# A two-layer decoder step on one core: sums of squared head outputs as two fp32r products, half tiles moved behind each output step, state buffers laid into dead memory, one subtraction moved ahead

## The chip, the cores and the metric

One core of a Trainium2 chip runs the whole program in one launch. The metric is device time in microseconds (us); each figure below is for that one core. The engines are named as the profile names them: PE is the matmul engine (PEld its weight loads), DVE the vector engine, ACT the scalar engine, POOL the general engine, SP the one that issues most loads.

## The reference

A decoder of two layers, each a half-step SwiGLU FFN, a mixer of three recurrent branches, and another half-step FFN. It is computed for one prompt of 512 tokens and for 8 running sequences of 4 new tokens, 544 token columns in all. The part of the mixer that the change touches:

```python
def head_rmsnorm(o, g):
    return o * lax.rsqrt(jnp.mean(o * o, axis=-1, keepdims=True) + EPS) * g

# per branch (HGRN2, GLA, mLSTM), 4 heads of 128 values each:
#   S_t = diag(exp(logf_t)) S_{t-1} + k_t v_t^T ;  o_t = S_t^T q_t
o_hg  = merge_heads(head_rmsnorm(o_hg,  g_hgrn)) * silu(hg)
o_gla = merge_heads(head_rmsnorm(o_gla, g_gla))  * silu(gg)
o_ml  = merge_heads(head_rmsnorm(h_ml,  g_ml))   * sigmoid(mo)
proj   = einsum('blcw,cwd->blcd', branches, w_branch[l])
merged = einsum('blcd,blcd->bld', sigmoid(mg), proj);  y = merged @ w_out[l]

def swiglu_half(x, g, w_up, w_down):
    gate, up = split(rmsnorm(x, g) @ w_up)
    return x + 0.5 * ((silu(gate) * up) @ w_down)
```

The running sequences bring a state (8 x 128 x 128 for each head of HGRN2 and mLSTM, two heads together for GLA), which is read, updated and written back.

## The kernel before

Activations lie transposed, 128 channels on the partitions and 544 token columns, which are treated as two halves of 272. **Dense products** (`dense`, L700) take three fp32r products for each 128x128 weight block: rounded weight by rounded activation, rounded weight by the activation's rest, the weight's rest by the rounded activation. A tile of the mixer has 8 blocks, so 48 matmuls of 272 columns; half a tile ("part") has 24. POOL splits each piece of weights into rounded part and rest (L567, L569), SP loads it. Two PSUM slots `dense` are used in turn; ACT or DVE empties a tile and gives its slot back (`slot_free`).

**The mixer's order** is one list, `ORDER`, that every engine walks. `mixer_order` makes it with `weave`: the recurrent steps of a branch, and behind each step so many half tiles of dense work as `HALVES_BEHIND` says (one row of numbers for each branch). PE starts a step only when DVE and ACT have finished the step before (`dve_step`, `act_step`); the half tiles between are the cover for their work. For each of 4 heads a branch ends with two steps:
- **o**, the output step: PE makes the head's outputs into PSUM `SA` (L972 to L976). ACT copies them to memory and squares them into `tmp[:, 2]` (L1355 to L1359). DVE makes `vblk` (L2028) and the next head's queries `qm` (L1913), and in the mLSTM branch adds a lower bound to the squares (L2037).
- **z**: PE makes the state update of the running sequences (L981, L984), then the sums of the squares over the 128 partitions by a product with `ones` in plain fp32 (L988), and, but for the last head, reads the next head's states (L817, L819). ACT takes Ln and Exp of the sums (L1382, L1385). DVE updates the state `sst` (L2042, L2044), then tells `dve_step`, then scales the outputs (L2050, L2052, L2054) with a copy by ACT between (L1394). DVE and ACT do all this in program order, and a gate's tile that ACT empties (L1260, Sigmoid) needs a table load before it, as Ln does after it.

That makes 24 o steps and 24 z steps (2 layers, 3 branches, 4 heads).

**States.** The 10 states of a layer pass through four buffers `sst0` to `sst3` (`st_buf`, `st_count`). A buffer is loaded again behind the o step once the store of its last state has landed.

**The start of an FFN** (f = 0 to 3, two for each layer). FFN 0 runs its tiles as dense products, with some replaced; FFNs 1 to 3 make nearly all tiles by seven half-size products (`fast`, L760), which need sums and differences of the activations: `combined` (L1601 to L1608), rounded by ACT (L1112, `combined_hi`) and their rest by DVE (L1612, `combined_lo`), in two groups, 0 and 1. PE's second product in `fast` waits for both rests. Between the two `combined_lo` DVE does `hidden_lo` (L1633) and `gate_scaled(2, 1)` (L1619), which empties PSUM slot 0 of the third tile. ACT's Silu (L1126) follows `gate_scaled`; then DVE `gate` (L1623) and `value` (L1628), ACT's copy to `Ah` (L1130), and ACT's copy of the first product (L1087), for which PE's fourth product waits. In FFN 0 the fifth tile of dense products uses slot 0 again.

Of the kernel before, what the change touches and what calls it, by code (L numbers as in the profile page):

```python
# [22 lines left out]
ALU = mybir.AluOpType  # L23
ACT = mybir.ActivationFunctionType

P = 128
# [76 lines left out]
def scan_steps(br):  # L103
# [135 lines left out]
def build(nc, wst, xT, par_d, lb_d, const_d, lvm_d, fg_d, st_h, st_g, st_c, st_n, st_m,  # L239
          yT, p_h, p_g, p_c, p_n, s_h, s_g, s_c, s_n, s_m, x_keep):  # L240
    ctx = ExitStack()
    with ctx:
        top = [(nc.sbuf_base + 31) // 32 * 32]

        def sb(name, shape, dt=F32, at=None):
# [3 lines left out]
            if at is None:  # L249
# [23 lines left out]
        tmp, tmp_at = sb("tmp", [P, 6, TOK])  # L273
        vblk, _ = sb("vblk", [2 * SMP, 512], at=tmp_at + 3 * TOK * 4)
# [29 lines left out]
        sst = [sb("sst0", [P, DEC_B, P])[0], sb("sst1", [P, DEC_B, P], at=tmp_at)[0],  # L304
               sb("sst2", [P, DEC_B, P], at=b_at + 4 * TOK * 4)[0], sb("sst3", [P, DEC_B, P], at=b_at + 6 * TOK * 4)[0]]
# [89 lines left out]
        den_sq, num_sq = sem("den_sq"), sem("num_sq")  # L395
        h_rs, h_of, h_hi, h_lo = sem("h_rs"), sem("h_of"), sem("h_hi"), sem("h_lo")
# [29 lines left out]
        def st_buf(n):  # L426

            return n % 2 if n < 7 else (2, 3, 1)[n - 7]

        def st_count(L, n):  # L430

            return L * (64, 64, 16, 16)[st_buf(n)] + 16 * (n // 2 + 1 if n < 7 else (1, 1, 4)[n - 7])
# [252 lines left out]
        def _(pe):  # L685
# [124 lines left out]
            def state_query(L, br, h, out):  # L810

                n = st_no(br, h)
                pe.wait_ge(st_in[st_buf(n)], st_count(L, n))
                pe.sem_inc(step_began, 1)
                for b in range(DEC_B):
                    j = b % 4
                    pe.matmul(out[j * SMP:(j + 1) * SMP, :], qm[:, b * SMP:(b + 1) * SMP], sst[st_buf(n)][:, b, :],  # L817
                              start=(b < 4), stop=(b > 4), skip_group_check=True)
# [11 lines left out]
            def step(L, s):  # L830
# [146 lines left out]
                elif kind == "z":  # L977
# [51 lines left out]
        def _(act):  # L1029
# [184 lines left out]
            def tile(L, t):  # L1214
# [42 lines left out]
                elif t in GATE_AT:  # L1257
                    m = GATE_AT[t][1]
                    tile_wait(L, t)
                    act.activation(halves(gates[:, m, :]), ps, ACT.Sigmoid).then_inc(free, 1)  # L1260

            def dma_state(L, i, store):
# [7 lines left out]
                if store:  # L1270
                    act.dma_start(v(d[0]), sst[st_buf(i)][:, :, :]).then_inc(st_out[st_buf(i)], 16)
                else:
                    act.dma_start(sst[st_buf(i)][:, :, :], v(d[1])).then_inc(st_in[st_buf(i)], 16)
# [15 lines left out]
            def step(L, s):  # L1289
# [31 lines left out]
                elif kind == "k":  # L1321
# [11 lines left out]
                    else:  # L1333
# [4 lines left out]
                        if br < 2:  # L1338
                            ch.did(act.activation(kts[:, 0:nt, :].rearrange("p a b -> p (a b)"),
                                                  SA[0:2 * SMP, 0, 0:nt * P], ACT.Copy))  # L1340
                elif kind == "ns":
# [8 lines left out]
                elif kind == "o":  # L1350
                    if br == 2:

                        act.activation(tmp[:, 2, 0:SEQ], SA[:, 0, :], ACT.Square).then_inc(num_sq, 1)
                        act.activation(tmp[:, 2, SEQ:TOK], SA[:, 1, 0:SMP], ACT.Square).then_inc(num_sq, 1)
# [7 lines left out]
                    n = st_no(br, h)  # L1362
# [4 lines left out]
                    if (br, h) == (1, 3):  # L1367
# [914 lines left out]
```

## Time and profile before

| | us |
|---|---|
| median of 3 runs | 2925.52 |
| lowest, highest | 2921.17, 2928.85 |
| the profiled execution | 2927.8 |
| its span, first to last instruction | 2926.0 |
| PE busy in the span | 2893.3 |
| DVE busy | 1634.6 |
| POOL busy | 1589.8 |
| ACT busy | 925.9 |

The span is cut into work of the engines. PE is busy nearly throughout, the others half the time or less. The mean granted clock of PE was 0.994 of full speed. The views used below are the page, the waits (who waited for whom), the timeline (instructions in order of time, alike ones merged), the list of a line's instructions, the windows (busy time of each engine in a stretch, with the granted clock) and the chain of work that ended last.

### The profile page before, as it was taken

The page shows a single profiled execution, that of the slowest core. Times are in us where ns is not written, and L with a number is a line of the kernel's source. Part 1 is how long each engine was busy: PE and PEld are TensorE (multiplying, and loading weights), DVE is VectorE, ACT ScalarE, POOL GpSimd, SP SyncE. Part 2 cuts the span into 40 slices and gives each one's busy share as a digit, 9 for nine tenths or more (in the row PEclk, how much of TensorE's full clock was granted, in tenths as well). Part 3 has the DMA queues.
Part 4 walks back from the last instruction along what each step waited for, and adds up shares of the span by engine and source line. Part 5 has one row for each costly group of instructions (what it writes and reads, how often), then busy time and mean ns, then how long its engine had stood idle before and what let it go on. Part 6 is the DMA issues. An engine that isn't in the chain of part 4 may idle for free.

```text
span 2926.0 us, 59967 instructions
## 1 busy us (share of the span) xinstructions
PE 2893.3 (99%) x23276; PEld 2817.1 (96%) x23276; DVE 1634.6 (56%) x2333; ACT 925.9 (32%) x1556; POOL 1589.8 (54%) x1466
## 2 busy tenths in 40 slices
PE   7999999999999999999999999999999999999998
PEld 7999999999989999999999999999999999999998
DVE  8563676543443577373784737755444336783745
ACT  4221233022142325252452514321312413351423
POOL 6676676555554574525465243755555546734343
PEclk9999999999999999999999999999999999999999
DMA  5796835465555554353444433464665556543532
GB/s 185 201 251 194 221 115 171 138 167 148 161 158 123 170 164 139 124 170 112 132 142 135 154 116 113 141 157 142 179 153 138 155 138 161 165 147 117 168 119 85
DMA packets 196941, 444.05 MB, mean 152 GB/s; under 512 B 13464, under 2 KB 57664, under 8 KB 195904
## 3 DMA queue, kind: packets, MB, share of 16 engines
q1 hardware_dynamic: 107360, 281.09, 29.6%
q0 software_dynamic: 40128, 125.83, 18.2%
q10 hardware_dynamic: 49248, 34.28, 3.9%
q8 instruction: 142, 2.33, 0.3%
q14 instruction: 63, 0.52, 0.1%
HBM read 422.64 MB, written 144.35 MB: 194 GB/s over the span
## 4 chain that ended last, share of the span: by engine, by line
PE 93%; DVE 4%; ACT 1%; DMA 1%; issue 1%; POOL 0%; DVEq 0%; ACTq 0%; SPq 0%; POOLq 0%
PE dense L700 58%; PE SA L760 14%; PE SB L760 11%; PE SA L901 1%; PE SA L988 1%; PE SA L887 1%; PE SA L828 1%; PE SA L972 1%; PE SB L984 1%; PE SA L975 1%; PE SA L872 0%; PE SA L817 0%; DVE TlH L1612 0%; ACT tx L1107 0%; PE SA L942 0%
## 5 line engine op out<-in xcount | busy, mean ns | idle before, releaser
L569 POOL TENSOR_TENSOR Wl<-raw,Wh 128x512 fp32r<-128x512 f32 x620 | 848.6, 1369 | 51.8
L567 POOL TENSOR_SCALAR Wh<-raw 128x512 fp32r<-128x512 f32 x620 | 450.2, 726 | 763.4 <-PEq L705 456.1
L700 PE MATMUL dense<-Hh,Wh 128*128 128x272 f32 x2784 | 590.2, 293 | 13.0 <-POOLq L571 10.5
L700 PE MATMUL dense<-Hh,Wl 128*128 128x272 f32 x2784 | 577.6, 289 | 0.0
L700 PE MATMUL dense<-Hl,Wh 128*128 128x272 f32 x2784 | 576.1, 289 | 0.0
L700 PEld LDWEIGHTS dense<-Hh,Wh 128*128 128x128 f32 x2784 | 438.2, 189 | 25.6 <-issue 19.1
L700 PEld LDWEIGHTS dense<-Hl,Wh 128*128 128x128 f32 x2784 | 439.3, 189 | 0.0
L700 PEld LDWEIGHTS dense<-Hh,Wl 128*128 128x128 f32 x2784 | 436.8, 190 | 0.0
L632 POOL TENSOR_TENSOR Sl<-pair,Sh 128x512 fp32r<-128x512 f32 x120 | 172.0, 1452 | 420.4 <-ACT Sh L1067 419.6
L700 PE MATMUL dense<-Ah,Wh 128*128 128x272 f32 x1408 | 292.6, 289 | 0.3 <-POOLq L571 0.2
L700 PE MATMUL dense<-Al,Wh 128*128 128x272 f32 x1408 | 291.1, 288 | 0.0
L700 PE MATMUL dense<-Ah,Wl 128*128 128x272 f32 x1408 | 289.9, 287 | 0.0
L700 PEld LDWEIGHTS dense<-Ah,Wh 128*128 128x128 f32 x1408 | 220.3, 188 | 1.5 <-issue 0.8
L700 PEld LDWEIGHTS dense<-Al,Wh 128*128 128x128 f32 x1408 | 221.6, 189 | 0.0
L700 PEld LDWEIGHTS dense<-Ah,Wl 128*128 128x128 f32 x1408 | 220.5, 189 | 0.0
L1766 DVE SCALAR_TENSOR_TENSOR X<-dense,X 128x544 f32 x64 | 46.4, 725 | 298.4 <-PE dense L700 297.9
L1067 ACT ACTIVATE Sh<-pair 128x512 fp32r<-128x512 f32 x240 | 144.4, 625 | 36.0 <-PE SA L760 35.8
L1067 ACT ACTIVATE Sh<-wsum 128x512 fp32r<-128x512 f32 x180 | 113.2, 630 | 100.2 <-PE SA L760 50.7
L1550 DVE TENSOR_TENSOR Sl<-wsum,Sh 128x512 fp32r<-128x512 f32 x180 | 133.5, 743 | 0.0
L1550 DVE TENSOR_TENSOR Sl<-pair,Sh 128x512 fp32r<-128x512 f32 x120 | 101.5, 846 | 12.7 <-ACT Sh L1067 12.7
L1087 ACT ACTIVATE tmp<-SA 128x272 f32<-128x272 f32 x60 | 22.8, 381 | 270.0 <-PE SA L760 270.0
L760 PE MATMUL SA<-ThH,Sh 128*128 128x272 f32 x320 | 92.8, 290 | 4.2 <-DVE TlH L1612 4.2
(457 smaller groups left out, 6321.2 us busy)
## 6 DMA issues: line engine op xcount, KB each, us to landing
raw<-wst SPq DMA_DIRECT2D x276, 512.0 KB, 3.6
w_sums<-wst POOLq DMA_DIRECT2D x36, 1536.0 KB, 13.1
w_sums<-wst POOLq DMA_DIRECT2D x18, 2048.0 KB, 15.7
pair<-wst SPq DMA_DIRECT2D x120, 256.0 KB, 3.5
pair<-w_sums SPq DMA_DIRECT2D x60, 512.0 KB, 3.7
wsum<-w_sums SPq DMA_DIRECT2D x60, 512.0 KB, 3.6
w_sums<-w_sums POOLq DMA_DIRECT2D x12, 1536.0 KB, 7.8
wsum<-wst SPq DMA_DIRECT2D x60, 256.0 KB, 2.5
```

The source lines that it names most:

```text
L567: pool.tensor_scalar(Wh[:, j, cs], raw[:, j, cs], 1.0, 0.0, ALU.mult, ALU.add).then_inc(glink, 1)
L569: pool.tensor_tensor(Wl[:, j, cs], raw[:, j, cs], f32(Wh[:, j, cs]), ALU.subtract).then_inc(glink, 1)
L632: pool.tensor_tensor(Sl[:, q, :], slot(q), f32(Sh[:, q, :]), ALU.subtract).then_inc(q_lo_pool, 1)
L700: mm = pe.matmul(dps[slot][:, a, 0:HALF], w[:, ring, w0:w0 + 128], x[:, k, a * HALF:(a + 1) * HALF], start=(k == 0 and n == 0), stop=(k == ...
L760: mm = pe.matmul(out, w[:, q, k * 128:(k + 1) * 128], xs[:, k, :], start=(opens and k == 0 and m == 0), stop=(k == 3 and m == 2), skip_gro ...
L828: return pe.transpose(out, in_, idn)
L887: mm = pe.matmul(o[s0:e, :, o0:o0 + n * hf].rearrange("p h (n b) -> p h n b", b=hf), K[:, kt(br, hh), c * CH + s0:c * CH + e], qs[:, :, s0 ...
L901: mm = pe.matmul(SA[:, hh // 2, col:col + 64], K[:, kt(br, hh), c * CH:(c + 1) * CH], q, start=True, stop=True)
L972: pe.matmul(SA[:, 0, cs], V[:, h, cs], att[:, h, cs], start=True, stop=(c == 0))
L1067: act.activation(Sh[:, q, :], slot(q), ACT.Copy).then_inc(q_hi, 1)
L1550: TT(Sl[:, q, :], slot(q), f32(Sh[:, q, :]), ALU.subtract).then_inc(q_lo, 1)
L1766: STT(xs, dps[j % 2][:, :, 0:HALF], 0.5, xs, ALU.mult, ALU.add).then_inc(slot_free[j % 2], 1)
```

## The change

The squares get a rounded part `sqh` (ACT copies `tmp[:, 2]` to fp32r) and a rest `sql` (DVE subtracts), and the sums are made by two fp32r products with `onesr` for each half of the columns. `HALVES_BEHIND` has now two half tiles behind every o step but one (three as before), and the z step gives what the o step gets. In pairs of (behind o, behind z) for heads 0 to 3 that is, before: HGRN2 (2,2) (1,2) (2,2) (1,4), GLA (1,2) (1,2) (1,2) (1,3), mLSTM (3,3) (1,3) (1,3) (1,3); and changed: HGRN2 (2,1) (2,1) (2,2) (2,4), GLA (2,1) (2,1) (2,1) (2,2), mLSTM (3,2) (2,2) (2,2) (2,3). ACT squares before it copies in all branches. The 10 states have 10 buffers, laid over `X`, `gates` and `setB` where these are dead, so that loads no longer wait for stores, and waits on stores move to those who write there next (ACT's gate tiles, DVE's `branch`). And `combined_lo(1)` stands right behind `combined_lo(0)`.

```diff
 HALVES_BEHIND = (
...
-    (1, 1, 1, 2, 4, 4, 2, 2, 2, 2, 2, 1, 1, 2, 1, 2, 1, 2, 1, 2, 1, 3),
+    (1, 1, 1, 2, 4, 4, 2, 2, 2, 2, 2, 1, 1, 2, 2, 1, 2, 1, 2, 1, 2, 2),
...
...
+        sqh, _ = sb("sqh", [P, TOK], F32R, tmp_at)
+        onesr, _ = sb("onesr", [P, P], F32R, tmp_at + TOK * 4)
+        sql, _ = sb("sql", [P, TOK], F32R, tmp_at + 2 * TOK * 4)
...
-        sst = [sb("sst0", [P, DEC_B, P])[0], sb("sst1", [P, DEC_B, P], at=tmp_at)[0],
-               sb("sst2", [P, DEC_B, P], at=b_at + 4 * TOK * 4)[0], sb("sst3", [P, DEC_B, P], at=b_at + 6 * TOK * 4)[0]]
+        st_at = ([X_at + 2 * n * TOK * 4 for n in range(4)] + [gates_at + n * TOK * 4 for n in (4, 6)]
+                 + [b_at + n * TOK * 4 for n in (4, 6, 12, 14)])
+        sst = [sb(f"sst{n}", [P, DEC_B, P], at=at)[0] for n, at in enumerate(st_at)]
... (PE, z step)
-                        mm = pe.matmul(SA[:, a, 0:HALF], ones[:, :], tmp[:, 2, a * HALF:(a + 1) * HALF],
-                                       start=True, stop=True)
+                        ts = slice(a * HALF, (a + 1) * HALF)
+                        pe.matmul(SA[:, a, 0:HALF], onesr[:, :], sqh[:, ts], start=True, stop=False)
+                        mm = pe.matmul(SA[:, a, 0:HALF], onesr[:, :], sql[:, ts], start=False, stop=True)
... (ACT, gate tiles)
+                    if GATE_AT[t] in ((1, 4), (1, 6)):
+                        n = m // 2 + 2
+                        act.wait_ge(st_out[n % 4], st_count(L, n))
... (ACT, o step)
+                    act.activation(tmp[:, 2, 0:SEQ], SA[:, 0, :], ACT.Square).then_inc(num_sq, 1)
+                    act.activation(tmp[:, 2, SEQ:TOK], SA[:, 1, 0:SMP], ACT.Square).then_inc(num_sq, 1)
                     ch.did(act.activation(O[:, h, 0:SEQ], SA[:, 0, :], ACT.Copy))
                     ch.did(act.activation(O[:, h, SEQ:TOK], SA[:, 1, 0:SMP], ACT.Copy))
-                    if br < 2:
-                        ch.did(act.activation(tmp[:, 2, 0:SEQ], SA[:, 0, :], ACT.Square))
-                        ch.did(act.activation(tmp[:, 2, SEQ:TOK], SA[:, 1, 0:SMP], ACT.Square))
+                    act.wait_ge(num_sq, idx * 2 + 2)
+                    if br == 2:
+                        act.wait_ge(num_den, L * HEADS + (h + 1))
+                    act.activation(sqh[:, :], tmp[:, 2, :], ACT.Copy).then_inc(sq_hi, 1)
                     ch.sync()
+                    act.wait_ge(sq_hi, idx + 1)
                     act.sem_inc(act_step, 1)
-                    if 0 < n < 7 and (br != 1 or h % 2 == 0):
-                        act.wait_ge(st_out[st_buf(n - 1)], st_count(L, n - 1))
-                        dma_state(L, n + 1 if n < 6 else 9, False)
+                    if (br, h) in ((0, 0), (0, 1)):
+                        dma_state(L, 2 + h, False)
... (DVE, start of an FFN)
                         combined_lo(0)
+                        combined_lo(1)
                         hidden_lo(f0, 0, slice(0, 1))
                         gate_scaled(2, 1)
-                        combined_lo(1)
                         gate(f0 + 1, 1)
... (DVE, o step; the mLSTM bound now comes before vblk and tells num_den)
+                    dve.wait_ge(sq_hi, idx + 1)
+                    ch.did(TT(sql[:, :], tmp[:, 2, :], f32(sqh[:, :]), ALU.subtract))
... (DVE, branch)
-                if br == 0 and m == 0:
-                    dve.wait_ge(x_store, L * 16 + 16)
+                if br == 0 and m % 2 == 0:
+                    dve.wait_ge(st_out[m // 2], st_count(L, m // 2))
```

PE, the first z step of the HGRN2 branch, before. One row of L988 stands for one fp32 matmul with `x2` for the two halves:

```order
L984 MATMUL SB<-vblk,kts 128x512 x2
L988 MATMUL SA<-tmp,ones 128x272 x2
L817 MATMUL SA<-sst_96,qm 32x128 x8
L819 MATMUL SA<-vts,att 32x128
L700 MATMUL dense<-Hh,Wh 128x272 x2
```

The same place in the changed kernel:

```order
L987 MATMUL SB<-vblk,kts 128x512 x2
L992 MATMUL SA<-sqh,onesr 128x272
L993 MATMUL SA<-sql,onesr 128x272
L992 MATMUL SA<-sqh,onesr 128x272
L993 MATMUL SA<-sql,onesr 128x272
L820 MATMUL SA<-sst_99,qm 32x128 x8
L822 MATMUL SA<-vts,att 32x128
```

Two fp32 matmuls have become four fp32r ones; what is before and behind them on PE is the same.

DVE at the start of FFN 0, before (the names ending in `M` are `H` in FFNs 1 and 3):

```order
L1612 TENSOR_TENSOR TlM<-tx,ThM 128x2176
L1633 TENSOR_TENSOR Al<-tmp,Ah 128x544
L1619 TENSOR_TENSOR tmp<-dense,tmp 128x544
L1612 TENSOR_TENSOR TlM<-tx,ThM 128x2176
L1623 TENSOR_TENSOR tmp<-tmp 128x544
L1628 TENSOR_TENSOR tmp<-dense,tmp 128x544
```

And changed:

```order
L1626 TENSOR_TENSOR TlM<-tx,ThM 128x2176 x2
L1647 TENSOR_TENSOR Al<-tmp,Ah 128x544
L1633 TENSOR_TENSOR tmp<-dense,tmp 128x544
L1637 TENSOR_TENSOR tmp<-tmp 128x544
L1642 TENSOR_TENSOR tmp<-dense,tmp 128x544
```

The second subtraction into `Tl` stands two instructions earlier, ahead of the one that empties PSUM slot 0 (L1619 before, L1633 now).

ACT from the first z step's last copy to the second z step, HGRN2 branch, before:

```order
L1394 ACTIVATE ohA<-setA 128x544
L1260 ACT_TABLE_LOAD
L1260 ACTIVATE gates<-dense 128x544
L1355 ACTIVATE setA<-SA 128x512
L1356 ACTIVATE setA<-SA 128x32
L1358 ACTIVATE tmp<-SA 128x512
L1359 ACTIVATE tmp<-SA 128x32
L1273 DMA sst_95<-st_h 128x8x128
L1294 ACT_TABLE_LOAD
```

And changed:

```order
L1409 ACTIVATE ohA<-setA 128x544
L1365 ACTIVATE tmp<-SA 128x512
L1366 ACTIVATE tmp<-SA 128x32
L1367 ACTIVATE setA<-SA 128x512
L1368 ACTIVATE setA<-SA 128x32
L1373 ACTIVATE sqh<-tmp 128x544
L1281 DMA sst_101<-st_h 128x8x128
L1268 ACT_TABLE_LOAD
L1268 ACTIVATE gates<-dense 128x544
L1302 ACT_TABLE_LOAD
```

The gate tile with its table load has moved behind the o step here, since only half a tile is left ahead of it, and the copy into `sqh` has come in.

## Rows read from the trace of the kernel before

**Rows 1.** The page, busy time and share of the span.
```profile
PE 2893.3 (99%) x23276; PEld 2817.1 (96%) x23276; DVE 1634.6 (56%) x2333; ACT 925.9 (32%) x1556; POOL 1589.8 (54%) x1466
```
**Rows 2.** Waits of PE: line, who was waited for, us, times, longest.
```profile
PE SA L760 <- DVE TlH L1612: 4.2, 2, 2.1
...
PE SA L760 <- DVE TlM L1612: 1.1, 1, 1.1
...
PE SA L817 <- DMA sst<-st_h: 0.7, 2, 0.4
```
**Rows 3.** Line L988, min/median/max ns of a record; two records for each matmul.
```profile
L988 PE MATMUL SA<-tmp,ones x96: 392/393/498, 630.6 to 2460.3; 128*128 128x272 f32 x96
```
**Rows 4.** Timeline of PE, first z step: start us, us, line, count.
```profile
629.25 0.41 PE L700 MATMUL dense<-Hh,Wl 128*128 128x272 f32 x2
629.59 1.13 PE L984 MATMUL SB<-vblk,kts 32*128 32x512 f32 x4
630.65 1.19 PE L988 MATMUL SA<-tmp,ones 128*128 128x272 f32 x4
631.76 0.64 PE L817 MATMUL SA<-sst,qm 128*32 128x128 f32 x16
...
632.66 0.52 PE L700 MATMUL dense<-Hh,Wh 128*128 128x272 f32 x2
633.02 0.41 PE L700 MATMUL dense<-Hl,Wh 128*128 128x272 f32 x2
```
**Rows 5.** Chain that ended last: start us, us, what; dense products without a wait.
```profile
67.62 12.03 PE dense L700 x96
79.64 3.04 PE SA L760 x24
```
**Rows 6.** Timeline, start of FFN 0, DVE and PE (idle before, in brackets).
```profile
43.56 0.71 DVE L1619 TENSOR_TENSOR tmp<-dense,tmp 128x544 f32<-128x544 f32 x1
44.20 2.86 DVE L1612 TENSOR_TENSOR TlM<-tx,ThM 128x2176 fp32r<-128x2176 f32 x1
...
44.43 0.51 PE L700 MATMUL dense<-Hh,Wh 128*128 128x272 f32 x2 [0.63 <-DVE tmp L1619]
```
**Rows 7.** Windows: stretch, busy time and count by engine; granted clock (PEclk) third from last.
```profile
1126.00:1130.00 4.00, 1.89 (x12) 1.68 (x11) 3.61 (x3) 0.39 (x2) 0.00 (x0) 0.86 0.00 0
1130.00:1134.00 4.00, 4.00 (x25) 4.00 (x25) 1.76 (x3) 2.52 (x6) 1.57 (x1) 0.71 0.10 18
...
2572.00:2576.00 4.00, 4.00 (x35) 4.00 (x34) 2.09 (x5) 3.09 (x7) 1.69 (x2) 1.00 0.05 17
```
**Rows 8.** Timeline, start of FFN 1, DVE and ACT.
```profile
1125.36 2.88 DVE L1612 TENSOR_TENSOR TlH<-tx,ThH 128x2176 fp32r<-128x2176 f32 x1
1128.17 0.71 DVE L1623 TENSOR_TENSOR tmp<-tmp 128x544 f32<-128x544 f32 x1
...
1125.48 0.66 ACT L1126 ACTIVATE tmp<-tmp 128x544 f32<-128x544 f32 x1 [3.10 <-DVE tmp L1619]
...
1130.31 0.38 ACT L1087 ACTIVATE tmp<-SA 128x272 f32<-128x272 f32 x1
```
**Rows 9.** Timeline behind the z step of rows 4: PE, DVE, ACT.
```profile
638.77 0.61 PE L972 MATMUL SA<-att,setA 128*128 128x128 f32 x4
...
640.48 0.50 PE L700 MATMUL dense<-Hh,Wh 128*128 128x272 f32 x2
...
634.03 1.22 DVE L2044 TENSOR_TENSOR sst<-sst,SB 128x1024 f32<-128x1024 f32 x1
...
638.99 0.73 DVE L2054 TENSOR_TENSOR olA<-setA,ohA 128x544 fp32r<-128x544 f32 x1 [0.72 <-ACT ohA L1394]
...
641.82 0.23 ACT L1359 ACTIVATE tmp<-SA 128x32 f32<-128x32 f32 x1
```
**Rows 10.** Lines L2054 and L2042, DVE: min/median/max ns.
```profile
L2054 DVE TENSOR_TENSOR olB<-kbuf,ohB x8: 724/1010/1709, 812.1 to 2293.4; 128x544 fp32r<-128x544 f32 x8
...
L2042 DVE TENSOR_TENSOR sst<-sst,decs x24: 1217/1225/1228, 632.8 to 2460.8; 128x1024 f32<-128x1024 f32 x16, 64x1024 f32<-64x1024 f32 x8
```

More of the change, by code:

```diff
@@ L395, in build @@
         den_sq, num_sq = sem("den_sq"), sem("num_sq")
+        num_den, sq_hi = sem("num_den"), sem("sq_hi")
         h_rs, h_of, h_hi, h_lo = sem("h_rs"), sem("h_of"), sem("h_hi"), sem("h_lo")
@@ L424, in st_no @@
             return h if br == 0 else 4 + h // 2 if br == 1 else 6 + h
-        def st_buf(n):
-            return n % 2 if n < 7 else (2, 3, 1)[n - 7]
+        st_all = (3, 3, 2, 2)
         def st_count(L, n):
-            return L * (64, 64, 16, 16)[st_buf(n)] + 16 * (n // 2 + 1 if n < 7 else (1, 1, 4)[n - 7])
+            return L * 16 * st_all[n % 4] + 16 * (n // 4 + 1)
         w_sums = nc.dram_tensor("w_sums", (4, (2 * DEPTH - 1) * FAST, P, 512), F32, kind="Internal").ap()
@@ L812, in state_query @@
                 n = st_no(br, h)
[L813 removed]
+                pe.wait_ge(st_in[n % 4], st_count(L, n))
                 pe.sem_inc(step_began, 1)
@@ L816, in state_query @@
                     j = b % 4
-                    pe.matmul(out[j * SMP:(j + 1) * SMP, :], qm[:, b * SMP:(b + 1) * SMP], sst[st_buf(n)][:, b, :],
+                    pe.matmul(out[j * SMP:(j + 1) * SMP, :], qm[:, b * SMP:(b + 1) * SMP], sst[n][:, b, :],
                               start=(b < 4), stop=(b > 4), skip_group_check=True)
@@ L1270, in dma_state @@
                 if store:
-                    act.dma_start(v(d[0]), sst[st_buf(i)][:, :, :]).then_inc(st_out[st_buf(i)], 16)
+                    act.dma_start(v(d[0]), sst[i][:, :, :]).then_inc(st_out[i % 4], 16)
                 else:
-                    act.dma_start(sst[st_buf(i)][:, :, :], v(d[1])).then_inc(st_in[st_buf(i)], 16)
+                    act.dma_start(sst[i][:, :, :], v(d[1])).then_inc(st_in[i % 4], 16)
             def gate_weights(L):
@@ L1340, in step @@
                                                   SA[0:2 * SMP, 0, 0:nt * P], ACT.Copy))
+                elif kind == "lv" and br == 1 and h in (5, 6):
+                    g = MIX_T0 + TILE_AT["b", 0, KT - 1]
+                    act.wait_ge(slot_free[g % 2], ONE + TILE_BASE[L] // 2 + (g // 2 + 1))
+                    dma_state(L, h - 1, False)
                 elif kind == "ns":
@@ L1433, in _ @@
                         if s[1] == GV:
-                            for g in (MIX_T0 + GV - 2, MIX_T0 + GV - 1):
-                                act.wait_ge(slot_free[g % 2], ONE + TILE_BASE[L] // 2 + (g // 2 + 1))
+                            act.wait_ge(x_store, L * 16 + 16)
+                            dma_state(L, 0, False)
                             dma_state(L, 1, False)
@@ L1994, in step @@
                 elif kind == "k":
+                    if (br, h) == (0, 0):
+                        ch.did(dve.tensor_copy(onesr[:, :], ones[:, :]))
                     if h == 0:
@@ L2027, in step @@
                 elif kind == "o":
+                    idx = L * 12 + (br * 4 + h)
+                    if br == 2:
+                        g = slice(h * SMP, (h + 1) * SMP)
+                        dve.wait_ge(num_sq, idx * 2 + 2)
+                        STT(tmp[g, 2, :], wrow[g, :], HUGE, tmp[g, 2, :], ALU.min, ALU.add).then_inc(num_den, 1)
                     ch.did(TT(vblk[:, :].rearrange("p (b v) -> p b v", v=P),
@@ L2040, in step @@
                     n = 64 if br == 1 else P
-                    st = sst[st_buf(st_no(br, h))]
+                    st = sst[st_no(br, h)]
                     ch.link(TT(st[sl], st[sl],
```

24 lines of the change are left out of this document (11 added, 13 removed), and 4 rows, old and new, of the table HALVES_BEHIND.

## The prediction

> **What bounds the kernel now.** The page comes first: PE is busy 99% of the span, the others 56% or less [rows 1]. So time falls only where PE works less or waits less, and rises wherever the change makes PE wait. The waits of PE come next [rows 2]: there are few. Those that this change can touch are the wait for `combined_lo(1)` at the start of FFNs 1 to 3 (4.2 us in two, 1.1 us in one) and two waits for a state load, 0.7 us together. The timeline of the z step then shows what the removed product costs PE [rows 4], the timelines of the FFN starts what surrounds the moved subtraction [rows 6, 8], and that behind the z step how late DVE and ACT are when PE comes back [rows 9]. The sum below is made against the profiled execution (span 2926.0 us, with what lies around it 2927.8) and is carried over to the median of 2925.5.
>
> **The product of the sums.** From the first record of L988 to the first of L817 PE needs 631.76 - 630.65 = 1.11 us [rows 4]; there are 24 such steps (96 records, four for each step [rows 3]). The new form is what a dense product is: a 272-column fp32r matmul every 12.03 / 96 = 0.125 us [rows 5]. Two edges cost extra. Behind another kind of product the first pair of dense matmuls takes 633.02 - 632.66 = 0.36 instead of 0.25 us, and from the last dense pair to L984 it is 629.59 - 629.25 = 0.34 instead of 0.25 [rows 4]. So the new step takes 4 x 0.125 + 0.11 + 0.09 = 0.70 us. The gain is 0.41 us x 24 = **9.9 us**, all of it on PE. It could be 0.5 us each (12 us) if the edges are free, and nothing if the four keep the present pace; I take 0.41, since `dense` is the same form.
>
> L2054 on DVE, a subtraction of the same shape as the new `sql`, shows 724 to 1709 ns [rows 10], and that range is used below. The Trainium skill, page "GPSIMD Engine Reference", gives a reason in section "1. Specifications": that engine's SBUF interfaces are shared with VectorE, and an instruction with two SBUF inputs contends there. The rule speaks against this change, which adds 24 such subtractions beside POOL's splits. By it each would take its long form of 1.7 us where it meets one of POOL's; by the short form it is 0.7 us. Where that could reach PE is worked out under the joints.
>
> **The states.** With a buffer of its own state 2 is loaded behind the first o step, some 17 us before PE needs it; the two waits go: **0.7 us** [rows 2]. Other loads sit beside work of 8 us and more. The loads cost ACT only issue time, no PE time. The new waits on stores are for stores issued at least a tile and a step earlier; if one were late, ACT's gate tiles would queue behind it. I take zero for them.
>
> **The moved subtraction, FFN 0.** There PE waits for L1619, `gate_scaled(2, 1)`, already: 0.63 us, and starts 0.15 us behind it [rows 6]. The change puts the second L1612 (2.86 us [rows 6]) ahead of L1619. Nothing else hides it, since the fifth tile needs PSUM slot 0; and nothing takes it back: two tiles of dense work, 12 us [rows 5], stand between this point and the first product that needs the rests. So PE's wait grows to 3.5 us: **a loss of 2.9 us**. On top comes the clock. In FFN 1, behind a PE wait of 2.1 us [rows 2], the granted clock shows 0.86 and then 0.71 as a mean over 4 us, which is a stretch at 1.2 GHz and the rest at 2.4 GHz, and PE starts 25 matmuls in the second 4 us; in FFN 3, behind a wait of the same length, it stays at 1.00 and PE starts 35 [rows 7]. Ten matmuls of 0.125 us are 1.25 us in that window alone, and the stretch begins ahead of it: I take 1.5 us for one fall. A wait of 3.5 us is longer than both, so I expect a fall: **a loss of 1.5 us**, with zero as the other end.
>
> The Trainium skill, "TensorE: Matmul & The Clock Gate", section "HAM oscillation — how this bites in real kernels", says that idle gaps between bursts of matmuls put the array back to half rate. By that rule alone the fall in FFN 0 is certain; by the rows the 2.1 us waits show it once in two. With the fall the whole sum is 6.4 us gained, without it 7.9.
>
> **The moved subtraction, FFNs 1 to 3.** PE's second product will start 1.7 us earlier in FFNs 1 and 3 and without a wait in FFN 2. But its fourth product waits for ACT's L1087, at the end of a chain: L1619, Silu on ACT (0.66 us), L1623, L1628, ACT's copy, L1087. Before, the Silu ran beside the second L1612 (from 1125.48, the subtraction until 1128.24), and L1623 started at 1128.17 [rows 8]. After, L1619 itself ends about 1128.2, and the Silu stands in the open: L1623 starts 0.8 us later, and L1087 ends not at 1130.69 but at 1131.5. The fourth product now starts three products (3 x 1.52 us [rows 5]) behind the first; before it started about 1131.6, when nothing but the clock held it, and after it can start at 1131.7. So the wait doesn't go; it moves from the second product to the fourth. I count 0.1, 0.3 and 0.1 us: **a loss of 0.5 us**. The one wait of 2.1 us is cut into 0.4 and 1.8, so the fall of the clock in FFN 1 should be gone: **1.5 us gained** against this profile.
>
> **The joints.** (a) *Behind z.* In ten places (five a layer) one half tile stands behind z where two stood. PE is back after 24 x 0.125 + 0.1 = 3.1 us. DVE tells `dve_step` when L2044 has ended, at 635.25, 2.6 us behind the start of the dense work at 632.66 [rows 4, 9]; with about 0.25 us to reach PE (0.15 in rows 6, and DVE's own wait on L2044) that leaves 0.25 us to spare. L2042 has shown 1217 to 1228 ns in all 24 [rows 10], so I count no wait. (b) *Behind o.* Added are ACT's copy of 544 columns (0.66 us, as L1126's of that size [rows 8]) and DVE's subtraction (0.7 to 1.7 us). With one half tile before they would not fit; with two, PE is back 6.2 us after it left o. Without a backlog they are done after about 1.3 + 0.7 + 1.7 + 0.3 = 4.0 us. With one half tile behind z, the backlog counts from z: PE is back at 3.1 + 1.7 (o step, 640.48 - 638.77 [rows 9]) + 6.2 = 11.0 us. ACT, with a gate tile's table load between, was done with the squares 642.05 - 632.66 = 9.4 us after z [rows 9]; the copy, the subtraction and the way to PE bring 11.0 to 12.1. That holds in four places, and in the six others DVE's own queue (L2054 ends at 7.1 [rows 9], and `vblk` and `qm` stand before the subtraction) is about as late as PE. I count 0.2 us in four places: **0.8 us lost**, with 0 and 13 us as the ends (four times 1.1, six times 0.2, ten times 0.7 where a subtraction of POOL's holds up L2042).
>
> **Sum.** -9.9 - 0.7 + 2.9 + 1.5 + 0.5 - 1.5 + 0.8 = **-6.4 us**, which is 2919.6 within the span and 2919 on the median: 0.22% faster. A measurement of this kernel tells a change of about 0.3%, 8.8 us, from none.
>
> **Rivals.**
> 1. *The moved subtraction pays.* If PE's slot in FFN 0 comes free in time, or the later products don't wait for the Silu chain, the waits of rows 2 go: 1.7 + 1.1 + 1.7 + 1.5 us instead of the loss. Sum -9.9 - 0.7 - 6.0 + 0.8 = -15.8: **2910**. For it speaks that PE's only named wait there is L1612; against it the bracket in rows 6. Chance 0.13.
> 2. *DVE and ACT bound the heads.* If most joints wait as in the upper end of (b), 13 us instead of 0.8: **2931**. It would take POOL's splits to meet nearly every new subtraction. Against it: L2042 never did. Chance 0.08.
> 3. *The product gets dearer, slower than before.* The change would not do what it says if the four fp32r products, pairs of them into one place of PSUM, ran one after the other with nothing overlapped, each at the 0.39 us that a record of L988 lasts [rows 3]: 4 x 0.39 + 0.2 = 1.8 us instead of 0.70, 26 us more in all: **2945**. It decides from 1.33 us a step on (15.2 us more over 24 steps), where the total passes +0.3%. Against it: L760 puts 12 in a row into one place, 24 in 3.04 us [rows 5]. Chance 0.03. If the four only keep the present pace, the sum is +3.5, **2929**, chance 0.03.
>
> **How the numbers follow.** My forecast and its near variants have 0.73; their range is 2913 to 2926 (no fall of the clock, free edges and no joints at one end, a few us of joints and a second fall at the other). About 0.12 of it lies below 2916.7, the bound for faster. With rival 1 that is 0.25 for faster. Slower takes rival 3's first form and the far tail of rival 2, together with a few late stores: 0.07. The rest, 0.68, is no change that can be told. The range for 8 in 10 is 2910 to 2929: it takes in rival 1 at one end and half of rival 2 at the other.
>
> **What would show it.** The z step from its first product of the sums to the state query: 0.70 us, 24 times. No wait of PE for `sst`. In FFN 0 a wait of PE of 3.5 us for the line that empties slot 0 at 47 us, with a granted clock below 1 just behind it. In FFNs 1 and 3 a wait of 0.4 us at the second product and one of 1.8 us at the fourth, on ACT's copy of the first product. Waits of PE at o steps: none; at z steps: a few tenths. Wrong is the argument if the fifth tile of FFN 0 starts at 44.4 us as before, if waits of a microsecond stand at the joints, or if the four products take anything but 0.7 us.

## Result and the profile after

| | before | changed |
|---|---|---|
| median, us | 2925.5 | 2937.3 |
| lowest, highest | 2921.2, 2928.9 | 2933.9, 2940.0 |
| the profiled execution | 2927.8 | 2937.3 |
| its span | 2926.0 | 2935.5 |

Each was timed in five runs. The change makes the kernel slower by 11.8 us: ratio 1.0042, interval 1.0031 to 1.0053. The forecast was 2919, range 2910 to 2929. So nearly 18 us are missing, and the profile after shows most of them at two places which the prediction had set to zero.

The waits of PE in the changed kernel (line, who was waited for, us, times, longest), to be held against [rows 2]:

```profile
PE SA L820 <- DMA sst<-st_h: 7.4, 2, 3.9
PE SA L763 <- ACT tmp L1091: 6.5, 3, 2.2
PE dense L703 <- DVE tmp L1633: 4.4, 2, 4.0
PE SA L975 <- issue: 2.7, 2, 1.5
...
PE SA L763 <- DVE TlH L1626: 0.8, 2, 0.4
```

L820 is the state query (L817 before), L763 `fast`, L1091 ACT's copy of the first product, L1633 `gate_scaled`, L1626 `combined_lo`, L975 the o step's first product. The third, second and last line were forecast. The first and fourth were not.

**The product.** Timeline of PE, the first z step after, against [rows 4]:

```profile
642.56 0.39 PE L992 MATMUL SA<-sqh,onesr 128*128 128x272 f32 x1
642.79 0.29 PE L993 MATMUL SA<-sql,onesr 128*128 128x272 f32 x1
642.92 0.29 PE L992 MATMUL SA<-sqh,onesr 128*128 128x272 f32 x1
643.04 0.28 PE L993 MATMUL SA<-sql,onesr 128*128 128x272 f32 x1
643.26 0.64 PE L820 MATMUL SA<-sst,qm 128*32 128x128 f32 x16
```

From L992 to L820 it takes 643.26 - 642.56 = 0.70 us where it took 1.11, as forecast. That holds in the 18 steps that end with a state query (before, two of them took 1.5 us, with the old state waits in them). In the six steps of a last head the next dense product starts 0.61 us behind L992 where it started 0.82 us behind L988. PE's later steps show that each of the 24 gives about 0.42 us.

**FFN 0.** DVE and PE, against [rows 6]; the second subtraction now lies ahead of L1647 and L1633. L1647 is `hidden_lo`, L1633 in the kernel before, where DVE showed

```profile
42.51 1.13 DVE L1633 TENSOR_TENSOR Al<-tmp,Ah 128x544 fp32r<-128x544 f32 x1
```

and in the changed kernel

```profile
42.53 2.83 DVE L1626 TENSOR_TENSOR TlM<-tx,ThM 128x2176 fp32r<-128x2176 f32 x1
45.29 1.78 DVE L1647 TENSOR_TENSOR Al<-tmp,Ah 128x544 fp32r<-128x544 f32 x1
46.99 0.71 DVE L1633 TENSOR_TENSOR tmp<-dense,tmp 128x544 f32<-128x544 f32 x1
...
47.85 0.81 PE L703 MATMUL dense<-Hh,Wh 128*128 128x272 f32 x2 [4.03 <-DVE tmp L1633]
```

The wait is 4.03 us, not 0.63: 3.4 us more. Behind it the clock is at its lower level, 1.2 GHz. So it is behind the wait for the state (windows; the third column from the right is the granted clock):

```profile
46.75:53.58 6.83, 5.73 (x25) 5.74 (x26) 4.85 (x6) 1.31 (x2) 4.66 (x4) 0.50 0.27 80
613.36:620.19 6.83, 5.69 (x36) 4.96 (x37) 0.00 (x0) 0.75 (x2) 3.79 (x4) 0.50 0.20 55
```

In the first, 25 matmuls take 5.73 us instead of 25 x 0.125 = 3.1: 2.6 us lost.

**The state.** The text on the change does not name one move that it contains: state 0, whose buffer now lies over `X`, is no longer loaded at the start of the mixer.

```diff
                 act.dma_start(m0[:, :], st_m[L, :, :]).then_inc(m_in, 16)
-                dma_state(L, 0, False)
                 for s in ORDER:
...
                         if s[1] == GV:
 
-                            for g in (MIX_T0 + GV - 2, MIX_T0 + GV - 1):
-                                act.wait_ge(slot_free[g % 2], ONE + TILE_BASE[L] // 2 + (g // 2 + 1))
+                            act.wait_ge(x_store, L * 16 + 16)
+                            dma_state(L, 0, False)
                             dma_state(L, 1, False)
```

ACT now issues the loads of states 0 and 1 together behind tile `GV` (issue column ACTq), shortly after POOL has issued a copy of weight sums from memory to memory (POOL L603). State 0 is needed at the first k step, PE's product L820:

```profile
598.45 1.49 POOL L603 DMA_DIRECT2D w_sums<-wst  x1 [0.78 <-POOL Wl L572]
...
601.17 1.39 ACTq L1281 DMA_DIRECT2D sst<-st_h  x2
...
614.50 1.08 PE L820 MATMUL SA<-sst,qm 128*32 128x128 f32 x16 [3.52 <-DMA sst<-st_h]
```

The DMA issues of 595 to 616 us, with KB each and the median from issue to landing:

```profile
w_sums<-wst POOLq DMA_DIRECT2D x1, 1536.0 KB, 15.1
raw<-wst SPq DMA_DIRECT2D x2, 512.0 KB, 5.5
sst<-st_h ACTq DMA_DIRECT2D x2, 512.0 KB, 13.7
```

The loads land 13.7 us after their issue (median of the two), PE stands for 3.5 us, in the second layer for 3.9, and runs at half clock afterwards. In the kernel before, state 0 was loaded at the start of the mixer, at 435.5 us, 165 us earlier.

**The second o step.** ACT and PE behind o(0,0), that is the first head's o step:

```profile
637.41 0.37 ACTq L1281 DMA_DIRECT2D sst<-st_h  x1
637.82 7.40 ACTq L1393 DMA_DIRECT2D p_h<-kbuf  x4
645.27 0.63 ACT L1268 ACTIVATE gates<-dense 128x544 f32<-128x544 f32 x1 [7.95 <-issue]
...
647.21 0.71 ACT L1397 ACTIVATE tmp<-SA,epsc 128x544 f32<-128x544 f32 x1
...
648.92 0.68 PE L975 MATMUL SA<-att,setA 128*128 128x128 f32 x4 [1.49 <-issue]
```

The four small stores of `p_h` took ACT 7.4 us to issue; before it was 1.90 us for the same four (ACT's timeline at 624.97). ACT's Ln (L1397) is late by that, and PE waits 1.49 us, in the second layer 1.22. The view names no releaser for this wait ("issue"); that the stores make it is shown by e5 and e9 below.

**FFNs 1 to 3.** DVE, ACT and PE in FFN 1, against [rows 8]:

```profile
1134.60 1.80 DVE L1647 TENSOR_TENSOR Al<-tmp,Ah 128x544 fp32r<-128x544 f32 x1
...
1137.07 0.66 ACT L1130 ACTIVATE tmp<-tmp 128x544 f32<-128x544 f32 x1 [6.52 <-DVE tmp L1633]
...
1139.91 0.38 ACT L1091 ACTIVATE tmp<-SA 128x272 f32<-128x272 f32 x1
...
1140.34 0.39 PE L763 MATMUL SA<-Mh,Sh 128*128 128x272 f32 x1 [2.17 <-ACT tmp L1091]
```

The wait has gone from the second product to the fourth, as forecast, by way of the Silu (L1130).

**The books.** Each matmul of one trace is paired with its counterpart in the other, start against start; the two profiled executions differ by +9.5 us. The product gives 10.0 us and the old state waits 0.8. FFN 0 costs 5.7 (6.0 at first, 3.4 of wait and 2.6 of half clock, of which 0.3 comes back later), FFNs 1 to 3 together 0.9, and the second o step 3.1. State 0 costs 13.3: 7.4 are PE's two waits, some 5 are half clock behind them, and the rest is that the query's first matmul, which before ran beside the product ahead of it, no longer does. Two falls of the clock go the other way: at 1883 us and at 2368 us the kernel before has stretches at 1.2 GHz which in the changed kernel's trace are missing or shorter, 3.0 us in all. That adds to 9.2; 0.3 us is spread thinly. The changed kernel's part in those 3.0 us is not shown: near 1883 us (1879 to 1891) e4, e8 and e10 have such a stretch, the other versions have none.

### The profile page after: what moved, and what is told of

Read it like the earlier page. It is cut to its first block, busy times and chain, and to the rows that moved or that the text cites. A ratio compares the mean times of both kernels' runs of the same rounds, so it can differ in the third digit from the quotient of the medians.

```text
span 2935.5 us, 60037 instructions
## 1 busy us (share of the span) xinstructions
PE 2887.6 (98%) x23276; PEld 2815.9 (96%) x23276; DVE 1639.6 (56%) x2359; ACT 939.2 (32%) x1580; POOL 1595.3 (54%) x1466
## 3 DMA queue, kind: packets, MB, share of 16 engines
q8 instruction: 142, 2.33, 0.3%
## 4 chain that ended last, share of the span: by engine, by line
PE 93%; DVE 4%; DMA 1%; ACT 1%; issue 1%; ACTq 0%; POOL 0%; DVEq 0%; SPq 0%; POOLq 0%
PE dense L703 59%; PE SA L763 14%; PE SB L763 10%; PE SA L904 1%; DMA sst<-st_h 1%; PE SA L890 1%; PE SA L975 1%; PE SA L831 1%; PE SB L987 1%; PE SA L978 1%; PE SA L820 0%; PE SA L875 0%; DVE TlH L1626 0%; DVE TlM L1626 0%; PE SA L992 0%
## 5 line engine op out<-in xcount | busy, mean ns | idle before, releaser
L1091 ACT ACTIVATE tmp<-SA 128x272 f32<-128x272 f32 x60 | 22.9, 381 | 270.1 <-PE SA L763 270.1
L1647 DVE TENSOR_TENSOR Al<-tmp,Ah 128x544 f32 (+1 forms) x88 | 72.1, 819 | 44.6 <-ACT Ah L1107 22.1
```

The lines of the kernel that those rows point to most:

```text
L1647: TT(Al[:, at, :], tmp[:, j:j + 1, :], f32(Ah[:, at, :]), ALU.subtract).then_inc(ffn_lo, 1)
```

## The experiments

Each version was timed beside the kernel before, whose medians were 2924.5, 2924.35 and 2924.4 in the three sets. The changed kernel was timed only beside the 2925.5 of the result. So distances between versions are taken here from their distances to the kernel before, which is +11.8 us for the changed kernel. Each such distance has an interval of about 3 to 5 us to either side.

**e1, the second subtraction back.** The changed kernel with this:

```diff
                         combined_lo(0)
-                        combined_lo(1)
                         hidden_lo(f0, 0, slice(0, 1))
                         gate_scaled(2, 1)
+                        combined_lo(1)
```

> The changed kernel with combined_lo(1) back in its old place, behind hidden_lo and gate_scaled; everything else stays changed. My theory, from the two traces matched matmul by matmul: the moved subtraction costs 3.4 us of wait and 2.9 us of half clock in FFN 0, gives 1.2 us in FFN 1 and takes 0.6 and 0.2 us in FFNs 2 and 3, so undoing it gives 5 to 7 us back: 2937 becomes 2931, and PE's wait in FFN 0 is 0.6 us again. Rival, the subtraction move is paid back elsewhere and the loss is all in the mixer: 2937 stays.

Measured: 2929.4, ratio 1.0015 (1.0005 to 1.0025), 4.9 us slower than the kernel before. So the move costs 11.8 - 4.9 = 6.9 us, of the size expected. The waits for the state are still there (7.5 us in two).

**e2, states 0 and 1 early.** The changed kernel with both loads behind tile `HF`, 130 us earlier:

```diff
-                        if s[1] == GV:
+                        if s[1] == HF:
                             act.wait_ge(x_store, L * 16 + 16)
                             dma_state(L, 0, False)
                             dma_state(L, 1, False)
```

> The changed kernel, but states 0 and 1 of each layer are loaded behind the ACT work of the first forget-gate tile (tile 9 of the mixer) and not behind that of tile 25; the moved subtraction stays. My theory: the two waits of PE for state 0 (3.5 and 3.9 us) go, and with them the two stretches at 1.2 GHz behind them (2.7 and 2.3 us): 12 us less, 2925. Rival, the stretches of low clock belong to the small matmuls of that step and not to the wait: only 7 us less, 2930, and the clock still falls there.

Measured: 2923.6, ratio 0.9995 (0.9985 to 1.0005), 0.9 us faster than the kernel before. 12.7 us come back; the wait list has no line for `sst` any more, and at the FFNs it is that of the changed kernel:

```profile
PE SA L763 <- ACT tmp L1091: 6.4, 3, 2.2
PE dense L703 <- DVE tmp L1633: 4.0, 1, 4.0
```

**e3, the subtraction alone.** The kernel before with `combined_lo(1)` moved, nothing else (the diff of e1 the other way round).

> The kernel before with combined_lo(1) moved right behind combined_lo(0), and nothing else of the change. My theory: 6 us slower than before (2931 to 2932), a PE wait of about 4 us in FFN 0 with a fall of the clock behind it, and in FFNs 1 to 3 a short wait at the second product and 2.1 us at the fourth, on ACT's copy of the first product. Rival, as in my prediction: 3 to 4 us slower, since one fall of the clock costs only 1.5 us. A third view, that the moved subtraction pays: 4 us faster.

Measured: 2934.9, ratio 1.0029 (1.0017 to 1.0041), 10.4 us slower. The part that was meant to shorten a wait is a loss by itself. It is 3.5 us more than e1 gives, which the intervals do not tell apart; in the traces the clock is a part of it: here the waits of 2.1 to 2.2 us at the fourth product are followed by a fall in all three FFNs, in the changed kernel's profile in none.

**e4, both.** The edits of e1 and e2 together.

> The changed kernel with both edits together: combined_lo(1) in its old place and states 0 and 1 loaded behind tile 9. What is left of the change is the fp32r product of the sums, the half tiles and the ten state buffers. If the two losses are independent they add: 18 us less than the changed kernel, 2919, that is 6 to 7 us faster than before. The product gives 10 us, the two old state waits 0.8, and what is still lost is two waits at the second output step of the first branch (1.5 and 1.2 us, behind slow issues of stores on ACT). Rival, a shared cause: less than the sum, 2924 or more.

Measured: 2916.3, ratio 0.9971 (0.9959 to 0.9982), 8 us faster than the kernel before. 6.9 + 12.7 = 19.6 us against 20.0 together: the two causes add up, as far as the intervals tell.

**e8, state 1 early, state 0 in its place.** This asks why state 0 lands late: because two loads go out together, or because of the time at which they go.

```diff
                         if s[1] == GV:
...
                             act.wait_ge(x_store, L * 16 + 16)
                             dma_state(L, 0, False)
+                        if s[1] == HF:
+
+                            act.wait_ge(x_store, L * 16 + 16)
                             dma_state(L, 1, False)
```

> The changed kernel (2937.3 us) with state 1 loaded behind tile HF and state 0 alone behind tile GV at its place. It tells apart why state 0 lands 13 us after its issue. Theory: the two loads, issued within 0.5 us of each other, share the queue; alone state 0 lands in 6 to 8 us, 607 to 609, before the k step at 611, so the waits of 3.5 and 3.9 us and the falls behind them go: 2937 - 13 = 2924. Rival: at that time any load of this size takes 13 us because other transfers run (state 1 alone took 13.1 us at 595.5 in the kernel before): the waits stay at 3 to 4 us, 2936.

Measured: 2938.0, ratio 1.0047 (1.0030 to 1.0064): nothing comes back. The theory of the shared queue fell. Alone state 0 lands 13.3 us after its issue, and PE waits for it as before, 3.6 and 3.8 us (DMA issues, 595 to 616 us):

```profile
w_sums<-wst POOLq DMA_DIRECT2D x1, 1536.0 KB, 15.2
raw<-wst SPq DMA_DIRECT2D x2, 512.0 KB, 5.8
sst<-st_h ACTq DMA_DIRECT2D x1, 512.0 KB, 13.3
```

The neighbour that is left is POOL's copy. The kernel before has the contrast too. Its load of state 1 behind `GV`, at 595.53, beside a copy in flight from 592.7 to 607.8, and its state load at 642.16, after one such copy had landed (638.9) and before the next began (644.7), took this long:

```profile
sst<-st_h ACTq DMA_DIRECT2D x1, 512.0 KB, 13.2
```

```profile
sst<-st_h ACTq DMA_DIRECT2D x1, 512.0 KB, 3.9
```

Twelve traces (all but e9) hold 240 state loads. A load issued with more than 5 us of such a copy still to come lands after 6.8 to 15.2 us, median 13.9 (38 loads); with no copy running or starting before it lands, 41 of 45 take 3.9 to 5.3 us, and the other four, 11.3 to 11.7 us, are issued right behind ACT's store of all of `X`. The other 157, with less of a copy to come or with one that starts meanwhile, take 3.9 to 14.8 us.

**e9, a short copy.** The changed kernel with that copy cut to 8 of 128 partitions. It leaves out the rest of one weight sum, so what FFNs 1 to 3 compute is wrong.

```diff
-                    pool.dma_start(W2, blocks[0, 0], accum_op=ALU.add).then_inc(sum_up[c], 16)
+                    pool.dma_start(W2[0:8], blocks[0, 0][0:8], accum_op=ALU.add).then_inc(sum_up[c], 16)
```

> The changed kernel (2937.3 us) with one of POOL's eight kinds of memory-to-memory copies of weight sums (the one that adds to the second sum, 1.5 MB, in flight at 598.5 to 613.6, 633.0 to 651.6, 2041.2 to 2056.3 and 2076.3 to 2094.6 in the changed kernel's trace) cut to 8 of its 128 partitions; the sums of FFNs 1 to 3 are wrong by what it leaves out. Theory: a state load lands late (13 to 15 us) only because that copy fills the DMA engines. Then states 0 and 1 land in 4 to 8 us, before PE comes at 611, the waits of 3.5 and 3.9 us and the falls behind them go; state 2's load lands in 4 to 6 us, the issue of the p_h stores behind it falls from 7.4 to about 2 us, and the two waits at the second o step go: 2937 - 13 - 2.5 = 2921 to 2922. Rival: the loads are slow for what they are (two of 512 KB in small pieces, or read behind stores) and the p_h stores are held up by the load itself: the landings and the waits stay, 2937.

Measured: 2923.05, ratio 0.9991 (0.9982 to 1.0001), 1.4 us faster than the kernel before: 13.2 us come back. The waits at L820 and L975 are both gone. The loads are issued within 0.3 us of where they were:

```profile
raw<-wst SPq DMA_DIRECT2D x3, 512.0 KB, 3.4
sst<-st_h ACTq DMA_DIRECT2D x2, 512.0 KB, 5.6
w_sums<-wst POOLq DMA_DIRECT2D x1, 96.0 KB, 4.7
```

So the copy is the cause of the late loads. It is of the held-up stores too: ns to issue one (min/median/max), the changed kernel, then e9:

```profile
L1393 ACTq DMA_DIRECT2D p_h<-kbuf x8: 610/1786/3129, 637.8 to 2086.8; - x8
```

```profile
L1393 ACTq DMA_DIRECT2D p_h<-kbuf x8: 453/508/1947, 631.3 to 2069.1; - x8
```

The Trainium skill, page "DMA: Bandwidth & Descriptors", sections "Queues, rings and completion order" and "Issuing engines are not separate DMA queues", says that transfers of all issuing engines run on the same 16 DMA engines, each of which takes turns between its queues by whole packets. By that rule a load shares with a copy. The runs agree, and give the size: 13.7 us to landing against 5.6. What exactly the two share is not shown. SP's loads (`raw`), of 512 KB too, took 5.5 us beside the same copy against 3.4 in e9, so the copy held them up far less than the state loads; no run here tells why.

**e5, four states early.** e4, with states 2 and 3 loaded behind tile `HF` too.

```diff
-                            dma_state(L, 0, False)
-                            dma_state(L, 1, False)
+                            for n in range(4):
+                                dma_state(L, n, False)
...
-                    if (br, h) in ((0, 0), (0, 1)):
-                        dma_state(L, 2 + h, False)
-                    elif (br, h) == (1, 0):
+                    if (br, h) == (1, 0):
```

> Starts from the version with both edits (second combined_lo back in its old place, states 0 and 1 loaded behind tile HF), 2916.3 us. States 2 and 3 are now loaded there too, and no load stands ahead of the p_h stores at o(0,0). Theory: at o(0,0) ACT loses about 5.5 us because the issue of the four p_h stores is held up behind the load of state 2 (7.4 us instead of 1.9), and that makes the wait of PE at the second o step (0.9 and 1.4 us). Then the issue falls to about 2 us, both waits go and the time falls by about 2.3 us to 2914. Rival: the stores are held up by what the load queues carry anyway (weights, or the q, k, v stores), and the issue and the two waits stay: 2916.

Measured: 2914.5, ratio 0.9962 (0.9948 to 0.9976). Both waits at the second o step are gone, with the copy still running beside the stores, and the issue times are back:

```profile
L1391 ACTq DMA_DIRECT2D p_h<-kbuf x8: 368/454/496, 624.5 to 2062.4; - x8
```

So it takes both: a load ahead in ACT's own queue, and a copy that holds that load up. The kernel before says the same: its 1.90 us for the four stores stand at 624.97, beside a copy in flight until 638.9, with no load ahead of them. The gain over e4, 1.7 us, lies within the two intervals; the waits and issue times decide this one.

**e6, the old table of half tiles.** e4 with `HALVES_BEHIND` as before the change.

> Starts from the same version (2916.3 us) and puts the old table of half tiles back: one half tile behind o in ten of twelve steps of a layer's GLA and mLSTM branches and one of HGRN2, two or three behind z. Theory of the prediction: with one half tile, 3.1 us, behind o, ACT's copy and DVE's subtraction (4.0 us behind o without a backlog) don't fit: 0.9 to 1.9 us of wait at some 18 z steps, with falls of the clock behind some of them, so 16 to 35 us slower, 2932 to 2951. Rival: the copy and the subtraction start before the o step has ended, or overlap so well that 3.1 us are enough: under 5 us slower, 2921 or less, and the new table was not needed.

Measured: 2918.0, ratio 0.9979 (0.9970 to 0.9989), 1.8 us slower than e4, intervals overlapping. The prediction's reason for the new table fell: with one half tile behind o there are eight waits, all short, 3.4 us together.

```profile
PE SB L987 <- DVEq L2077: 3.4, 8, 0.7
```

A GLA head of e6, where there is no wait; PE's o step ends with L979, the z step begins with L984:

```profile
824.54 0.31 PE L979 MATMUL SA<-const,osb 128*128 128x32 f32 x2
827.87 1.07 PE L984 MATMUL SB<-vblk,kts 32*64 32x512 f32 x4
...
824.88 0.60 ACT L1365 ACTIVATE tmp<-SA 128x512 f32<-128x512 f32 x1 [2.55 <-PE SA L979]
...
826.01 0.68 ACT L1373 ACTIVATE sqh<-tmp 128x544 fp32r<-128x544 f32 x1
...
826.72 0.73 DVE L2056 TENSOR_TENSOR sql<-tmp,sqh 128x544 fp32r<-128x544 f32 x1 [0.68 <-ACT sqh L1373]
```

Squares, copy and subtraction end 827.45 - 824.85 = 2.6 us behind o, where the prediction had 4.0.

**e7 and e11, the Silu first.** e5, and in every FFN the order that lets the Silu run beside the second subtraction and empties the PSUM slot ahead of `hidden_lo`. e11 is the same kernel, measured again.

```diff
                         combined_lo(0)
-                        hidden_lo(f0, 0, slice(0, 1))
                         gate_scaled(2, 1)
                         combined_lo(1)
                         gate(f0 + 1, 1)
                         value(f0 + 1, 2, 1)
+                        hidden_lo(f0, 0, slice(0, 1))
                         hidden_lo(f0 + 1, 1, slice(1, 2))
```

> The version with four states early, and at the start of each FFN DVE does combined_lo(0), gate_scaled(2, 1), combined_lo(1), gate, value, hidden_lo(0), hidden_lo(1). Theory: gate_scaled comes 1.1 us earlier, so in FFN 0 the wait for slot 0 (0.63 us) goes; in FFNs 1 to 3 the second subtraction ends 1.0 us earlier, the wait at the second product is 1.1 us instead of 2.1 in two of them and near 0 in the third, and the chain by way of the Silu to the fourth product, which now has the Silu beside the second subtraction, comes no later than PE: 3.5 us less, and fewer falls of the clock: 2910 to 2912, if the four states give 2914. Rival: the third tile's sums are not ready that early or the fourth product waits for what the second no longer does: no gain, 2914.

> The version with four states loaded early and gate_scaled and the Silu ahead of the second subtraction once more, in five rounds, to narrow its interval: 2910 again, ratio 0.995, if the first measurement holds; 2914, as without the new order in the FFNs, if it was chance.

Measured: 2910.0, ratio 0.9951 (0.9934 to 0.9967), and again 2911.1, ratio 0.9955 (0.9940 to 0.9969). It is the fastest version of the study, 14.3 and 13.4 us below the kernel before. Against e5 that is a gain of 4.4 and 3.5 us, with overlapping intervals. The waits of e11 at these places:

```profile
PE SA L763 <- DVE tmp L1677: 1.5, 1, 1.5
PE SA L763 <- DVE TlH L1624: 1.2, 2, 0.6
```

2.7 us stand where e5 has 5.3 (4.2 for `TlH`, 1.1 for `TlM`). The wait at the second product in FFN 2 is gone, as expected, but the chain behind it is not free: the 1.5 us stand in FFN 2 at the fifth product, for a line of DVE (L1677) that two `hidden_lo` (2.33 us) and, in this FFN alone, a copy of the layer's constants now precede:

```profile
1494.50 1.25 DVE L1595 COPY par<-parL 128x31 f32<-128x31 f32 x1
1496.09 0.44 DVE L1677 TENSOR_TENSOR tmp<-SA,tmp 128x272 f32<-128x272 f32 x1 [0.34 <-DVE par L1595]
```

No fall of the clock is left in FFNs 1 to 3, where the trace of e5 has two.

**e10, FFN 0 alone.** The changed kernel with the second subtraction in its old place in FFN 0 only.

```diff
                         combined_lo(0)
-                        combined_lo(1)
+                        if L or which:
+                            combined_lo(1)
                         hidden_lo(f0, 0, slice(0, 1))
                         gate_scaled(2, 1)
+                        if not (L or which):
+                            combined_lo(1)
```

> The changed kernel (2937.3 us) with the second combined_lo back in its old place in FFN 0 alone; FFNs 1 to 3 keep it moved. Theory from the trace: of the 7.9 us that the move costs, FFN 0 has 6.3 (a wait of 4.0 us instead of 0.6, and a fall of the clock behind it): 2931.0, and FFNs 1 to 3 have the rest, 1 to 2 us. Rival: the cost lies in FFNs 1 to 3 as much, by falls of the clock behind their waits at the fourth product: 2934.

Measured: 2930.9, ratio 1.0018 (1.0008 to 1.0027), 6.5 us slower than the kernel before. Of the 6.9 us FFN 0 has 5.3; 1.6 us are left for FFNs 1 to 3. The waits say about the same: there PE waits 6.5 + 0.8 = 7.3 us in the changed kernel, and 5.3 us with the old order.

## Why the prediction was wrong, point by point

- **The product** (-9.9): right, 0.70 us wherever a state query follows, -10.0 over the 24 steps. Rival 3 is excluded by the same rows.
- **The states** (-0.7): the old waits did go. The step that failed is "Other loads sit beside work of 8 us and more", with "no PE time" for them. It gave a state load a span without asking for its time to landing. The kernel before had the number: its own load behind tile `GV`, at 595.5, landed 13.2 us later, and nobody waited for it, since it was state 1, not state 0. The change put state 0 there, with 10 us to go. Cost: 7.4 us of waits, 13.3 us with the half clock and the slow start behind them (12.7 in e2).
- **"The loads cost ACT only issue time"**: wrong as well. The issue time itself is not fixed: 7.4 us instead of 1.9, and 2.7 us of PE's waiting, 3.1 by the pairing. In the working of the joints ACT had no DMA at all, though one of the steps has five in a row.
- **FFN 0** (+2.9 and +1.5): mechanism and place right, both sizes too small. The wait is 4.0 us, not 3.5, since L1647 took 1.78 us behind the moved subtraction where it took 1.13 before. The fall cost 2.6 us: the one in FFN 1 from which the 1.5 was taken was a shorter stretch at 1.2 GHz than this one. 5.7 us against 4.4.
- **FFNs 1 to 3** (+0.5, -1.5): the shift to the fourth product is as described, 0.4 and 2.2 us where 0.4 and 1.8 stood, and the fall in FFN 1 (worth 1.5 us by the pairing too) is gone in the changed kernel's profile. But the shift costs more: in FFN 2 the wait went from 1.06 to 2.13 us where 0.3 us more was forecast, and in the other two PE waits 0.5 us more where 0.1 was. L1647, with 1.80 us instead of 1.13 in FFN 1, is part of it. +0.9 against -1.0. (The fourth product of FFN 1 before, "about 1131.6" in the prediction, started at 1133.1; the rest is the fall, which the prediction counts by itself.) That a fall is gone with the shorter wait was chance, though: e3 has three. Rival 1 is excluded: the moved subtraction doesn't pay, in e1, e3 and e10.
- **The joints** (+0.8, up to 13): none of the waits named came. DVE's subtraction `sql` took 705 to 840 ns in all 24 steps:

```profile
L2056 DVE TENSOR_TENSOR sql<-tmp,sqh x24: 705/725/840, 637.6 to 2463.9; 128x544 fp32r<-128x544 f32 x24
```

A subtraction of POOL, with two inputs in SBUF, ran beside 12 of them. Eight it covered for over half a us, and these took 705 to 728 ns; the six with nothing of POOL beside them took 724 to 726. The rule on shared SBUF interfaces that the prediction quoted from the Trainium skill ("GPSIMD Engine Reference", "1. Specifications") did not show here; the 1.7 us of [rows 10] was not the price. Rival 2 is excluded, and e6 shows that even the old table would have cost little, 1.8 us by the medians and 3.4 us by the waits.
- **The clock.** In all thirteen traces, 13 waits of 3.5 to 4.0 us at the places of this study were all followed by a stretch at 1.2 GHz (in some it had begun before the wait was over); of 28 waits of 2.0 to 2.2 us, 14 were; of 23 waits of 0.9 to 1.6 us, none. The prediction expected a fall in FFN 0 and took the waits of 2.1 us to show one "once in two"; both held. The rule quoted from the Trainium skill ("TensorE: Matmul & The Clock Gate") agrees with the long waits; which of the short ones are followed by a fall it does not tell.

Put together: -6.4, and to it +13.3 and +3.1 that were missing, +1.3 in FFN 0, +1.9 in the other FFNs, -0.2 for the product and the old waits and -0.8 for joints that did not wait, gives +12.2 us; with the 3.0 us of falls that only the trace before has it is +9.2 for the profiled executions, which show +9.5. The late load decided between slower and even (without it, e2 and e9 cannot be told from the kernel before), and the list of rivals had no case for it; the range reached 2929 and would have needed that case to hold 2937. The forecast gain came only with the subtraction put back as well: -8.2 us in e4.

## To carry to other kernels

When an edit moves a load, read how long a load of that size took from issue to landing at the new place, beside what else is on the DMA engines then, and hold it against the first reader; "nobody waits for it now" says nothing once another buffer is loaded there. DMAs that an engine issues belong into its chain of work with their issue time, which grows while a load ahead of them is held up. An instruction that is moved ahead to shorten one wait delays all that it is moved past: put first what frees a buffer or starts another engine's work, then the long one (such an order gained some 4 us by the medians, e7 and e11 against e5, where the moved subtraction alone cost 10, e3).

## What the runs showed of the hardware that was not expected

- A 512 KB load took 3.9 to 5.3 us to land, and 13.9 (median) with more than 5 us of a copy from memory to memory of 1.5 or 2 MB still to come; with the copy cut short two loads that had taken 13.7 took 5.6.
- Issuing a store of 64 KB took ACT 0.45 us, and up to 3.1 us with a held-up load ahead of it in ACT's queue.
- In the changed kernel's trace three waits of 3.5 to 4.0 us each had a stretch of 6.8 us at 1.2 GHz behind them, which cost 2.3 to 2.7 us more, two thirds of the wait once more. In four of the 13 such waits of all traces (two in e8, one each in e2 and e10) the stretch was half as long.
